# A 16x16 block inverse by substitution in place of four doubling levels, with its blocks moved through DRAM

## The chip, the cores and the metric

One core of one Trainium2 chip runs the whole program. The metric is the device time of one execution in microseconds (us). TensorE (PE) does matmuls and transposes, VectorE (DVE) and ScalarE (ACT) elementwise work, GpSimd (POOL) elementwise work and indirect transfers; SyncE (SP) issues most DMAs, ACT some. Each engine runs its own instruction stream in order and waits on semaphores.

## What is computed

One decoder layer for 512 prompt tokens and 32 sample tokens: an input projection, a gated DeltaNet branch, a forgetting-attention branch, gates and an output projection, and a mixture of 64 experts. The change is mostly in the DeltaNet recurrence over the prompt, in chunks of 64 tokens:

```python
lmat = beta[..., :, None] * jnp.einsum('nbhik,nbhjk->nbhij', k, k) * dec_strict
gam = jnp.exp(big_g)
rhs = beta[..., None] * jnp.concatenate([v, gam[..., None] * k], axis=-1)
sol = lax.linalg.triangular_solve(lmat, rhs, left_side=True, lower=True, unit_diagonal=True)
...
def step(s, xs):
    w1c, w2c, qgc, aqkc, kdc, glc = xs
    u = w1c - jnp.einsum('bhck,bhkv->bhcv', w2c, s)
    o = jnp.einsum('bhck,bhkv->bhcv', qgc, s) + jnp.einsum('bhij,bhjv->bhiv', aqkc, u)
    s = glc[..., None, None] * s + jnp.einsum('bhck,bhcv->bhkv', kdc, u)
    return s, o
```

`lmat` is strictly lower triangular, so the solve needs the inverse of a unit triangular 64x64 matrix for each chunk and head.

## The kernel before

The program is a row of blocks with a barrier of all engines between them. The block of the DeltaNet recurrence (L1347 and on, 447 to 761 us) works through four tiles of 128 tokens (two chunks each), all eight heads at once. For a tile, TensorE does in order:

- 16 transposes of keys and queries (L1362), the decay rows (L1367) and key-key and key-query products (L1371). DVE and ACT then make the decay matrix (L1486, L1544) and DVE the scaled matrix LT (L1492, L1493; its last write raises `lt_done`).
- The inverse, by doubling. `Um` holds the inverse of the diagonal blocks found so far and `Tm` its transpose. Level 0 (blocks of 2) needs one set of transposes (L1385); each of levels 1 to 5 (blocks of 4 to 64) masks LT on DVE (`level_mask`, L1475), multiplies it with Tm (L1393), lets ACT copy the product out of PSUM (L1561), multiplies with Um (L1403), lets DVE subtract (L1511), and, but for the last, transposes Um (L1411) for ACT to copy (L1564).
- The weighted rows w1 and w2 (L1417, L1418, in turns), and for each chunk the recurrence (L1431, L1437 to L1439) with DVE's updates (L1519 to L1522).

Between these steps stand "later pieces": parts of products that the next blocks need (the branch gates and later modulation rows), whose place is written out by hand in `later_pieces`. There are 80 in all, 12 of them in the block before. Of the 68 in this block 54 are halves of a gate group (L1202, four matmuls of 272 columns), 7 are raw modulation products (L1197) and 7 spread those over rows (L1189). ACT copies finished groups out of two banks (`later_out`: L1238, L1225, L1230) and stores them. Their weights come in 2 MB loads that SP issues (`send_later`, L226), each when an earlier slab has been used. POOL works on the sample tokens' state all the while (L1625 to L1635, until 607 us).

Other places that the change touches: the tile of 32 sample tokens of the z projection (L682, among the sample attention), the same tile in the shared expert (L2115), and the loads of the modulation rows (`load_mod`, L1762 and L1763).

## Time and profile before

| what | us |
|---|---|
| median of 3 runs | 1658.97 |
| lowest, highest run | 1651.38, 1660.43 |
| the profiled execution's own time | 1660.09 |
| its span in the trace | 1658.1 |
| TensorE busy | 1521.5 (92%) |
| VectorE, ScalarE, GpSimd busy | 615.4, 323.4, 316.8 |
| recurrence block, barrier to barrier | 447.2 to 761.1 |

The span is what the trace covers; the execution's own time is 2.0 us more. A fp32 matmul is listed as two instructions, so x16 beside a product of eight heads is eight matmuls. A row of the timeline that merges pipelined instructions ends a little after the next one starts; the step between starts is what a piece of work takes.

### The profile page before, as it was taken

The page shows a single profiled execution, that of the slowest core. Times are in us where ns is not written, and L with a number is a line of the kernel's source. Part 1 is how long each engine was busy: PE and PEld are TensorE (multiplying, and loading weights), DVE is VectorE, ACT ScalarE, POOL GpSimd, SP SyncE. Part 2 cuts the span into 40 slices and gives each one's busy share as a digit, 9 for nine tenths or more (in the row PEclk, how much of TensorE's full clock was granted, in tenths as well). Part 3 has the DMA queues.
Part 4 walks back from the last instruction along what each step waited for, and adds up shares of the span by engine and source line. Part 5 has one row for each costly group of instructions (what it writes and reads, how often), then busy time and mean ns, then how long its engine had stood idle before and what let it go on. Part 6 is the DMA issues. An engine that isn't in the chain of part 4 may idle for free. (4 is left out here: it accounts for less than half of the span.)

```text
span 1658.1 us, 21127 instructions
## 1 busy us (share of the span) xinstructions
PE 1521.5 (92%) x8094; PEld 886.0 (53%) x8094; DVE 615.4 (37%) x1260; ACT 323.4 (20%) x701; POOL 316.8 (19%) x345
## 2 busy tenths in 40 slices
PE   5999999999989899998998779999999989999966
PEld 3866767644677777787745333444343433333322
DVE  2002554331763625333669833421111111111128
ACT  1003334332331223221102201111111111111121
POOL 7000000000169971000002510111111111111000
PEclk8999999999999999998999899999999999999978
DMA  9312111112351143306540187999999999999665
GB/s 341 125 51 97 41 52 51 52 51 77 126 152 67 60 142 120 122 10 226 194 146 30 38 317 271 395 407 414 409 422 399 400 420 411 413 385 422 260 263 237
DMA packets 103231, 357.15 MB, mean 215 GB/s; under 512 B 27243, under 2 KB 27371, under 8 KB 77011
## 3 DMA queue, kind: packets, MB, share of 16 engines
q1 hardware_dynamic: 78998, 300.80, 47.0%
q0 software_dynamic: 15520, 39.17, 6.2%
q10 hardware_dynamic: 8614, 15.84, 2.7%
q8 instruction: 65, 1.06, 0.3%
q14 instruction: 34, 0.28, 0.0%
HBM read 330.70 MB, written 37.64 MB: 222 GB/s over the span
## 5 line engine op out<-in xcount | busy, mean ns | idle before, releaser
L1991 PE MATMUL bank<-arena 128*32 128x512 f32 (+2 forms) x1536 | 334.7, 611 | 23.5 <-DMA arena<-in_w_up 23.5
L1991 PEld LDWEIGHTS bank<-arena 128*32 128x32 f32 (+2 forms) x1536 | 119.1, 138 | 206.5 <-issue 206.2
L1999 PE MATMUL bank<-arena 128*32 128x512 f32 (+2 forms) x768 | 168.6, 598 | 0.7 <-DVE arena L2733 0.7
L2727 DVE TENSOR_TENSOR arena<-arena,bank 128x256 f32<-128x256 f32 x46 | 19.4, 421 | 324.0 <-ACT arena L2385 324.0
L1978 POOL DMA_INDIRECT expert_rows<-arena x46 | 46.5, 1010 | 486.0 <-PE bank L1984 419.5
L1202 PE MATMUL bank<-arena 128*128 128x272 f32 x512 | 129.7, 401 | 0.4 <-ACT arena L1238 0.4
L438 PE MATMUL bank<-arena 128*128 128x272 f32 x480 | 113.0, 398 | 4.7 <-DVE arena L1860 2.4
L1999 PEld LDWEIGHTS bank<-arena 128*32 128x32 f32 (+2 forms) x768 | 55.0, 134 | 110.3 <-issue 109.4
L1202 PEld LDWEIGHTS bank<-arena 128*128 128x128 f32 x512 | 94.7, 193 | 24.2 <-ACT arena L1238 3.8
L438 PEld LDWEIGHTS bank<-arena 128*128 128x128 f32 x480 | 92.1, 193 | 25.1 <-DVE arena L1860 3.2
L668 PE MATMUL bank<-arena 128*128 128x272 f32 x384 | 100.3, 405 | 0.0
L455 PE MATMUL bank<-arena 128*128 128x512 f32 (+3 forms) x304 | 84.8, 437 | 3.3 <-ACT arena L2331 2.4
L2385 ACT ACTIVATE arena<-bank 128x256 f32<-128x256 f32 x46 | 17.7, 384 | 347.5 <-PE bank L1991 347.5
L2739 DVE COPY arena<-bank 128x512 f32<-128x512 f32 x46 | 31.8, 692 | 126.8 <-PE bank L1999 126.8
L668 PEld LDWEIGHTS bank<-arena 128*128 128x128 f32 x384 | 70.2, 193 | 16.0 <-issue 3.6
L455 PEld LDWEIGHTS bank<-arena 128*128 128x128 f32 (+1 forms) x304 | 45.3, 187 | 41.4 <-issue 36.8
L1607 POOL TENSOR_TENSOR arena<-arena 128x512 f32<-128x512 f32 x5 | 6.8, 1354 | 290.5 <-POOLq L1243 290.2
L2447 POOL DMA_INDIRECT expert_lists<-arena x34 | 35.6, 1046 | 137.8 <-DVE arena L2573 128.4
L1984 PE MATMUL bank<-arena 128*128 128x128 f32 x368 | 49.5, 279 | 9.0 <-DMA arena<-h_rows,arena 9.0
L2391 ACT COPY arena<-bank 128x512 f32<-128x512 f32 x46 | 27.0, 587 | 152.4 <-PE bank L1999 152.4
L1974 POOL DMA_INDIRECT arena<-h_rows,arena x46 | 47.0, 1023 | 44.0 <-DVE arena L1918 24.0
L1393 PE MATMUL bank<-arena 128*128 128x128 f32 x320 | 42.1, 283 | 12.7 <-DVE arena L1508 7.4
(469 smaller groups left out, 2124.8 us busy)
## 6 DMA issues: line engine op xcount, KB each, us to landing
arena<-in_w_gate SPq DMA_DIRECT2D x64, 1024.0 KB, 12.5
arena<-in_w_up SPq DMA_DIRECT2D x64, 1024.0 KB, 16.6
arena<-in_w_down SPq DMA_DIRECT2D x64, 1024.0 KB, 15.5
arena<-in_w_ada SPq DMA_DIRECT2D x12, 2048.0 KB, 10.3
arena<-in_w_in SPq DMA_DIRECT2D x11, 2048.0 KB, 8.7
arena<-expert_rows SPq DMA_DIRECT2D x8, 2048.0 KB, 25.5
gate_logits<-arena ACTq DMA_DIRECT2D x16, 272.0 KB, 2.3
arena<-gate_logits SPq DMA_DIRECT2D x8, 544.0 KB, 5.2
```

Source lines behind the costliest of these rows:

```text
L438: mm = nc.tensor.matmul(pair[i][:, 0:HALF], w[:, k, m * P:(m + 1) * P], rhs[:, k, i * HALF:(i + 1) * HALF], start=k == 0, stop=k == kt - 1)
L455: mm = nc.tensor.matmul(out, lhs[:, k, t * P:t * P + n], w[:, k, cols], start=k == 0, stop=k == kt - 1)
L668: mm = nc.tensor.matmul(out[:, 0:HALF], w[:, k, (m % 4) * P:(m % 4 + 1) * P], hT[:, k, half * HALF:(half + 1) * HALF], start=k == 0, stop= ...
L1202: mm = nc.tensor.matmul(out[:, 0:HALF], w[:, k, m * P:(m + 1) * P], hT[:, k, half * HALF:(half + 1) * HALF], start=k == 0, stop=k == KD - 1)
L1393: mm = nc.tensor.matmul(bank[hb][:, col(h)], Lm[:, h, :], Tm[:, h, :], start=True, stop=True)
L1974: return nc.gpsimd.indirect_dma_start(out=into, out_offset=None, in_=h2_d, in_offset=bass.IndirectOffsetOnAxis(ap=rows, axis=0), bounds_ch ...
L1978: return nc.gpsimd.indirect_dma_start(out=y_d, out_offset=bass.IndirectOffsetOnAxis(ap=rows, axis=0), in_=of, in_offset=None, bounds_check ...
L1984: mm = nc.tensor.transpose(bank[half][:, k * P:(k + 1) * P], of[:, kk * P:(kk + 1) * P], ident)
L1991: mm = nc.tensor.matmul(out[rows].rearrange("p (a n) -> p a n", a=2), x[:, k, rows], gate_up_slot(n)[:, :, k, :], start=k == 0, stop=k == ...
L1999: mm = nc.tensor.matmul(out[rows, :], h[:, k, rows], down_slot(n)[:, k, 512 * half:512 * half + 512], start=k == 0, stop=k == 1)
L2447: scat.inc(nc.gpsimd.indirect_dma_start(out=list_rows, out_offset=bass.IndirectOffsetOnAxis(ap=adi[:, t, k:k + 1], axis=0), in_=tokval[:, ...
L2739: nc.vector.tensor_copy(Yb[u % RY][:, 512:D], bank[6][:, :]).then_inc(y_v.sem, 1)
```

## The change

- The masks for the levels (`lvl`, 24 GpSimd instructions) go. Levels 0 to 3 of the inverse go with them.
- In their place the eight diagonal blocks of 16x16 of LT, for eight heads, are inverted by forward substitution on DVE. For that the blocks are stored to DRAM (`key_blocks`: eight stores, the even blocks on SP's queue, the odd ones on ACT's), loaded back with one block and head per partition (two loads), and the result `x16` goes the same way back (two stores of `key_block_inverses`, eight loads into `Um`). The substitution is 15 steps of a product and a subtraction on `xp` in PSUM and one copy, 31 instructions, each waiting for the one before.
- Two levels stay (blocks of 32 and of 64). Their blocks of LT are copied by ACT into zeroed tiles instead of being masked on DVE.
- Keys and decays of tile t+1 are made before the weighted rows of tile t, and the substitution for tile t+1 stands between the two chunks of tile t on DVE. The 68 later pieces are placed anew.
- The decay rows use both halves of the array in turns; the weighted rows are eight matmuls of one kind and then eight of the other.
- Products for 32 tokens (z, the shared expert, the modulation rows) are done in four column groups of 32 rows instead of at 512 columns. The modulation rows go to DRAM unexpanded, and their loads take five DMAs instead of two; two of the four sets are issued by SP behind the first two gate loads instead of by ACT.

```diff
-    lvl = const(6, P)
+    gqT_odd, n16 = const(CW, P), const(16, 16)
...
+    n16_d = nc.dram_tensor("key_blocks", (NB, H, 16, 16), F32).ap()
+    x16_d = nc.dram_tensor("key_block_inverses", (NB, H, 2, 8, 16), F32).ap()
-    NL = 6
+    xp = bank[2][:, 0:128].rearrange("p (r i) -> p r i", r=8)
+    NL = 2
...
+            def block_inverses(t):
+                dve.wait_ge(xp_made.sem, t + 1)
+                dve.wait_ge(n16_in.sem, 32 * (t + 1))
+                for j in range(15):
+                    n = 15 - j
+                    row = xp[:, :, j:j + 1].to_broadcast([P, 8, n])
+                    step(nc.vector.tensor_tensor(p16[:, :, 0:n], row, n16[:, j:j + 1, j + 1:16].to_broadcast([P, 8, n]), ALU.mult))
+                    step(nc.vector.tensor_tensor(xp[:, :, j + 1:16], xp[:, :, j + 1:16], p16[:, :, 0:n], ALU.subtract))
+                done(x16_done, nc.vector.tensor_copy(x16[:, :, 1:16], xp[:, :, 1:16]))
...
+            later_pieces(pe, "state before", 2)
+            keys_and_decays(0)
+            for t in range(PT):
+                levels(t)
+                if t + 1 < PT:
+                    keys_and_decays(t + 1)
+                weighted_rows(t)
+                states(t, 0)
+                later_pieces(pe, (t, "state between"), (4, 4, 3, 1)[t])
+                states(t, 1)
...
+                for a in range(1, NB, 2):
+                    b16 = slice(16 * a, 16 * a + 16)
+                    n16_odd_out.inc(act.dma_start(n16_d[a].rearrange("h j i -> j h i"), LT[b16, :, b16]), 16)
...
+            def store_key_blocks(t):
+                sp.wait_ge(lt_done.sem, t + 1)
+                for a in range(0, NB, 2):
+                    b16 = slice(16 * a, 16 * a + 16)
+                    n16_out.inc(sp.dma_start(n16_d[a].rearrange("h j i -> j h i"), LT[b16, :, b16]), 16)
+            def load_key_blocks(t):
+                sp.wait_ge(n16_out.sem, 8 * NB * (t + 1))
+                sp.wait_ge(n16_odd_out.sem, 8 * NB * (t + 1))
+                for g in range(2):
+                    n16_in.inc(sp.dma_start(n16[64 * g:64 * g + 64], n16_d.rearrange("a h j i -> (a h) j i")), 16)
+            def move_block_inverses(t):
+                sp.wait_ge(x16_done.sem, t + 1)
+                for g in range(2):
+                    x16_out.inc(sp.dma_start(x16_d[:, :, g].rearrange("a h r i -> (a h) r i"), x16[64 * g:64 * g + 64]), 16)
+                sp.wait_ge(x16_out.sem, 32 * (t + 1))
+                for a in range(NB):
+                    b16 = slice(16 * a, 16 * a + 16)
+                    um_in.inc(sp.dma_start(Um[b16, :, b16], x16_d[a].rearrange("h g r i -> (g r) h i")), 16)
...
-                for k in range(KD):
-                    mm = nc.tensor.matmul(out, hT[:, k, t * P:t * P + n], ws[0][:, :, k, :], start=k == 0, stop=k == KD - 1)
+                for k in range(KD):
+                    for q in range(4) if t == PT else ():
+                        mm = nc.tensor.matmul(out[QUAD * q:QUAD * q + QUAD, 0:P], hT[:, k, SEQ:TOK], ws[0][:, q // 2, k, P * (q % 2):P * (q % 2) + P],
+                                              start=k == 0, stop=k == KD - 1)
```

The order on TensorE in one level of the inverse of a tile, before; four more such groups follow or precede it (L1393: product with Tm, L1403: with Um, L1202: a later piece, L1411: transposes of Um):

```order
L1393 MATMUL bank<-arena 128x128 [waits later_inverse_T_copied,level_masked]
L1393 MATMUL bank<-arena 128x128 x3
L1393 MATMUL bank<-arena 128x128 [waits later_inverse_T_copied,level_masked]
L1393 MATMUL bank<-arena 128x128 x3
L1403 MATMUL bank<-arena 128x128 [waits LT_product_copied]
L1403 MATMUL bank<-arena 128x128 x3
L1403 MATMUL bank<-arena 128x128 [waits LT_product_copied]
L1403 MATMUL bank<-arena 128x128 x3
L1202 MATMUL bank<-arena 128x272 [waits later_loaded1]
L1202 MATMUL bank<-arena 128x272 x3
L1411 MATMUL bank<-arena 128x128 [waits inverse_updated]
```

The order on TensorE now, where the second tile's inverse begins (line numbers are those of the changed kernel: L1198 and L1203 are later pieces, L1399 the transposes of Um, L1407 and L1412 the two products of a level):

```order
L1198 MATMUL bank<-arena 32x512 [waits later_loaded1,later_product_copied]
L1198 MATMUL bank<-arena 32x512 x7
L1203 MATMUL bank<-arena 128x272 [waits later_loaded0,later_product_copied]
L1203 MATMUL bank<-arena 128x272 x3
L1399 MATMUL bank<-arena 128x128 [waits o_copied,block_inverses_loaded]
L1399 MATMUL bank<-arena 128x128 x7
L1407 MATMUL bank<-arena 128x128 [waits inverse_T_copied,level_blocks_copied]
L1407 MATMUL bank<-arena 128x128 x3
L1407 MATMUL bank<-arena 128x128 [waits inverse_T_copied]
L1407 MATMUL bank<-arena 128x128 x3
L1412 MATMUL bank<-arena 128x128 [waits LT_product_copied]
L1412 MATMUL bank<-arena 128x128 x3
```

Five levels have become two, and the inverse starts with a wait for the loads of the block inverses, with two later pieces ahead of it.

On SP, the loads of weights (L227; L226 before) now stand between the small transfers. The first tile's part of the queue, where before were only the three L226 rows:

```order
L227 DMA arena<-in_w_in 128x8x512 [waits later_product]
L1667 DMA key_blocks<-arena 16x8x16 [waits LT_done]
L1667 DMA key_blocks<-arena 16x8x16 x3
L1673 DMA arena<-key_blocks 64x256 [waits odd_key_blocks_stored,key_blocks_stored]
L1673 DMA arena<-key_blocks 64x256
L227 DMA arena<-in_w_ada 128x8x512 [waits later_product] x2
L1678 DMA key_block_inverses<-arena 64x128 [waits block_inverses_done]
L1678 DMA key_block_inverses<-arena 64x128
L1682 DMA arena<-key_block_inverses 16x8x16 [waits block_inverses_stored]
L1682 DMA arena<-key_block_inverses 16x8x16 x7
L227 DMA arena<-in_w_in 128x8x512 [waits later_product]
```

Two weight loads stand between the block loads and the stores of the inverses, and each waits for a later piece on TensorE.

## Rows read from the trace of the kernel before

**Rows 1.** The page, part 1: busy us, share of the span, instructions.

```profile
PE 1521.5 (92%) x8094; PEld 886.0 (53%) x8094; DVE 615.4 (37%) x1260; ACT 323.4 (20%) x701; POOL 316.8 (19%) x345
```

**Rows 2.** Windows: the recurrence block; busy PE, PEld, DVE, ACT, POOL, clock, DMA.

```profile
447.20:761.10 313.90, 295.89 (x2208) 238.11 (x2208) 149.84 (x219) 82.80 (x184) 150.16 (x102) 0.97 0.28 91
```

**Rows 3.** Timeline of PE: start, duration, line; one level of the first tile.

```profile
481.77 2.02 PE L1393 MATMUL bank<-arena 128*128 128x128 f32 x16 [0.33 <-ACT arena L1564]
483.63 2.00 PE L1403 MATMUL bank<-arena 128*128 128x128 f32 x16
485.47 2.00 PE L1202 MATMUL bank<-arena 128*128 128x272 f32 x8
487.31 1.04 PE L1411 MATMUL bank<-arena 128*128 128x128 f32 x8
488.67 2.02 PE L1393 MATMUL bank<-arena 128*128 128x128 f32 x16 [0.33 <-ACT arena L1564]
```

**Rows 4.** Timeline of PE: the weighted rows' first and last, then chunk one.

```profile
508.12 0.43 PE L1417 MATMUL bank<-arena 128*128 128x64 f32 x2
...
513.94 2.10 PE L1202 MATMUL bank<-arena 128*128 128x272 f32 x8
515.97 0.68 PE L1431 MATMUL bank<-arena 64*64 64x64 f32 x16
...
520.62 2.10 PE L1202 MATMUL bank<-arena 128*128 128x272 f32 x8
```

**Rows 5.** Timeline of PE: the head of a tile, at full clock and after a wait.

```profile
454.16 2.05 PE L1367 MATMUL bank<-arena 8*128 8x128 f32 x16
456.14 2.00 PE L1371 MATMUL bank<-arena 64*128 64x256 f32 x16
458.07 5.77 PE L1202 MATMUL bank<-arena 128*128 128x272 f32 x24
...
530.91 3.65 PE L1362 MATMUL bank<-arena 128*128 128x128 f32 x16 [2.56 <-DVE arena L1526]
534.35 3.30 PE L1202 MATMUL bank<-arena 128*128 128x272 f32 x8
```

**Rows 6.** Timeline of DVE: from small to large instructions, and held ones.

```profile
432.74 0.19 DVE L1272 COPY arena<-bank 128x32 f32<-128x32 f32 x1
432.97 0.18 DVE L1273 TENSOR_SCALAR arena<-arena 128x32 f32<-128x32 f32 x1
...
464.50 0.43 DVE L1493 TENSOR_TENSOR arena<-bank,arena 128x256 f32<-128x256 f32 x1
...
469.30 4.00 DVE L1506 TENSOR_TENSOR arena<-arena 128x512 f32<-128x512 f32 x1
...
479.24 1.41 DVE L1475 TENSOR_TENSOR arena<-arena,bank 128x512 f32<-128x512 f32 x2
```

**Rows 7.** Timeline of SP: small stores, and the next load that waits for them.

```profile
447.44 8.33 SPq L1580 DMA_DIRECT2D sample_rows<-arena  x24
457.02 0.68 SPq L1586 DMA_DIRECT2D arena<-in_state_ssm  x1
```

**Rows 8.** DMA issues, 400 to 770 us: size each, median time to landing.

```profile
arena<-in_w_in SPq DMA_DIRECT2D x3, 2048.0 KB, 8.6
arena<-sample_out POOLq DMA_DIRECT2D x8, 8.0 KB, 2.1
arena<-in_x_sample SPq DMA_DIRECT2D x1, 128.0 KB, 13.5
sample_out<-arena POOLq DMA_DIRECT2D x2, 32.0 KB, 8.2
```

**Rows 9.** Timeline of PE: 32-token products at 512 columns, and in quarters.

```profile
407.54 3.62 PE L682 MATMUL bank<-arena 128*32 128x512 f32 x8
...
902.29 1.96 PE L448 MATMUL bank<-arena 128*32 128x128 f32 x64
...
973.00 7.05 PE L2115 MATMUL bank<-arena 128*32 128x512 f32 x16
```

More of the change, by code:

```diff
@@ L1064, in take_z @@
                 n, src = TOKS[t], filled(act, ("z", t))
-                read(("z", t), nc.scalar.activation(z_tm[0:n, t, :], src[0:n, :], ACT.Silu))
+                for rows, cols in QUARTERS if t == PT else [(slice(0, P), slice(0, W))]:
+                    ins = nc.scalar.activation(z_tm[0:n, t, cols], src[rows, 0:cols.stop - cols.start], ACT.Silu)
+                    ach.inc(ins) if cols.stop < W else read(("z", t), ins)
             for b in range(DB):
@@ L1188, in later_piece @@
             pe.wait_ge(fill_rd.sem, GROUP_OF[("raw", p[1])] + 1)
-            fill_mm.inc(nc.tensor.matmul(out[0:1 + NS_TOK, :], sel33, raw, start=True, stop=True))
+            for rows, cols in QUARTERS:
+                mm = nc.tensor.matmul(out[rows, 0:P], sel9, raw[:, cols], start=True, stop=True)
+            fill_mm.inc(mm)
             return
@@ L1373, in _, with levels @@
                 kk_mm.inc(mm)
-                later_pieces(pe, (t, "decay"), 3)
-                later_pieces(pe, (t, "masks"), 2)
+                later_pieces(pe, (t, "decay"), 14 if t == 0 else 4)
+            def levels(t):
+                later_pieces(pe, (t, "inverse back"), 2)
+                pe.wait_ge(um_in.sem, 16 * NB * (t + 1))
+                if t:
+                    pe.wait_ge(o_sb.sem, t)
+                for hb in range(2):
+                    for h in range(4 * hb, 4 * hb + 4):
+                        mm = nc.tensor.transpose(bank[hb][:, col(h)], Um[:, h, :], ident)
+                    t_mm.inc(mm)
@@ new lines, in _ @@
+            for i in range(2):
+                scaled_rows(0, i)
+            done(s_zero, nc.vector.memset(S, 0.0))
+            step(nc.vector.memset(Um, 0.0))
+            for Lm in Lm_of:
+                done(lm_zero, nc.vector.memset(Lm, 0.0))
+            for i in range(2, 5):
+                scaled_rows(0, i)
+            keys_and_decays(0)
+            dve.wait_ge(i16_made.sem, 2)
+            step(nc.vector.tensor_copy(x16[:, :, 0:1], i16[:, :, 0:1]))
+            block_inverses(0)
@@ new lines, in _ @@
+            for t in range(PT):
+                q = hd(qkv_tm[:, t, 0:W])
+                if t + 1 < PT:
+                    scaled_rows(t + 1, 0)
+                    scaled_rows(t + 1, 1)
+                inverse_level(t, 0)
+                if t + 1 < PT:
+                    for i in range(2, 5):
+                        scaled_rows(t + 1, i)
+                inverse_level(t, 1)
+                if t + 1 < PT:
+                    keys_and_decays(t + 1)
+                dve.wait_ge(w_mm.sem, t + 1)
+                done(w1_sb, nc.vector.tensor_copy(rows_of[t % 2][:, 0], bank[4].ap()))
+                if t + 1 < PT:
+                    step(nc.vector.memset(Um, 0.0))
+                states(t, 0)
+                if t + 1 < PT:
+                    block_inverses(t + 1)
+                states(t, 1)
@@ new lines, in _ @@
+            later_out(act, "state before")
+            keys_and_decays(0)
+            for t in range(PT):
+                if 0 < t < PT - 1:
+                    act.wait_ge(o_sb.sem, t)
+                    scales_to_psum(t + 1)
+                later_out(act, (t, "inverse back"))
+                take_T(t, 0)
+                take_P1(t, 0)
+                later_out(act, (t, "level"))
+                take_T(t, 1)
+                take_P1(t, 1)
+                if t + 1 < PT:
+                    keys_and_decays(t + 1)
@@ L1603, in _ @@
             step = chained(pool, gch)
+            for g in range(2):
+                half = i16[64 * g:64 * g + 64]
+                step(pool.memset(half, 0.0))
+                i16_made.inc(pool.affine_select(out=half, in_=half, compare_op=ALU.not_equal, fill=1.0, base=8 * g,
+                                                pattern=[[1, 8], [-1, 16]], channel_multiplier=0))
+            pool.wait_ge(i16_made.sem, 2)
             for t in range(NT):
```

350 lines of the change are left out of this document (180 added, 170 removed).

## The prediction, made before the changed kernel ran

> **What bounds the kernel now.** I read the shares first [rows 1]: TensorE is busy 92% of the span, the others 37% and less, so what counts is TensorE's own work and its waits. Then the window of the recurrence block [rows 2]: 313.9 us, TensorE busy 295.9, clock 0.97. The timeline shows what it does there. One level of the inverse goes from 481.77 to 488.67, 6.90 us [rows 3]: first product 1.86, second 1.84, a later piece 1.84, transposes and a short wait for ACT 1.36. Nothing in a level waits for long; DVE and ACT are hidden. So removed matmuls should show nearly in full, as long as what takes their place is hidden too.
>
> I count the block as work plus rest. Per tile: transposes 1.8, decay rows 1.98 and key products 1.93 [rows 5], first transposes 0.9, five levels of 3.70, four sets of transposes of 0.95, the weighted rows 5.82 (508.12 to 513.94), and twice 0.61 + 1.95 for the chunks (the gaps between pieces in [rows 4]): 39.8, four times is 159. The 68 later pieces: 54 at 1.84, 7 raw ones at 1.86, 7 of rows at 0.98, together 119. Work 278.6, so the rest (waits, half clock, tail) is 35.3 of the 313.9.
>
> **TensorE's work after.** Three of five levels go: 3 x (3.70 + 0.95) = 13.9 us per tile. The weighted rows take 0.364 per matmul in turns; alone, a product of eight takes 0.23 each [rows 3], and 16 of them 3.9: 1.9 saved (an estimate, since a change of tile shape is what I blame; between nothing and 3.0). The decay rows with both halves in turns: between 0 and 0.98 saved, I take 0.6, as 64-row products (L1371) do run two at a time, 256 columns in the time that 128 take alone. The seven row pieces become four matmuls in four column groups, about 0.3 instead of 0.98: 4.8 in all. Sum 4 x 16.4 + 4.8 = 70.4; work after 208.2.
>
> **The chain that replaces it.** From `lt_done` of a tile to its inverse on TensorE: four stores per queue at 0.35 each (8.33 for 24), 1.25 from the end of the last issue to the next instruction that waits for them [rows 7]; two loads 0.7 + 2.1, the landing of the small load [rows 8]; the substitution; two stores 0.7 + 1.3; eight loads 2.8 + 2.1. A DVE instruction costs 0.15 + 0.00104 per element (0.19 at 32 columns, 0.43 at 256, the gap to the next 0.04) [rows 6]. The 30 of the substitution have 8n elements, n from 15 to 1, twice 960 in all: 2.0 + 30 x 0.19, and the copy 0.3, 8.1 us (bound: 12, if such short strided forms take 0.4 each). The Trainium skill (DMA: Bandwidth & Descriptors, "Anatomy of one DMA") puts the fixed cost of any DMA at about 2.0 us, mostly the receipt of the write. By it both store legs would be 0.7 longer and the sum about 6 us higher; the store row here says 1.25, the load row agrees.
>
> The substitution of tile t+1 stands on DVE behind the first chunk of tile t, so it starts when that is done, about 10.3 after `lt_done` (3.9 + piece + 0.61 + 1.84 + 1.95 + DVE), when its blocks have long arrived (5.5). It ends at 18.4, its result is back at 25.3. TensorE in that time has weighted rows 3.9, two chunks of 2.56, and 9 later pieces, 25.0 together. So the chain is just covered: a wait of 1 us per tile. DVE is in the substitution when the second chunk's product comes, at 0.1, 1.3 and 2.9 us too late where 4, 4 (one short) and 3 pieces stand between: 4.3. A step of one store less in issue (ACT takes the odd ones) is 1.4 us per tile on a leg that has 4.8 us to spare: nothing.
>
> **The first tile is the weak place.** Its chain starts at TensorE's key products plus 6.9 (458.07 to 464.93 [rows 5, 6]), beside 14 pieces. ACT empties the banks of the pieces only after its four stores and seven copies, about 4.3 us after `lt_done`, while TensorE runs out of free banks after 3 pieces: a wait of 7.7. The weights of the fifth raw piece are loaded only after the block loads are issued: 8.6 us [rows 8], a wait of 3.2. The next slab's load goes out when that piece is done, and the stores of the inverses are queued behind its 2 MB: the small load behind a big one took 13.5 [rows 8]. I get the inverse back 5.7 after TensorE is ready. After a wait of 2.56 the next 24 instructions took 6.95 instead of 3.97 [rows 5], at the clock's lower level, so I add 3.0 once, behind the 5.7; behind the two other waits the chain hides it.
>
> Rest after: first keys 1.2, banks 7.7, slab 3.2, inverse of the first tile 5.7 and clock 3.0, copies inside the levels 4 x 1.0, `lt_done` and subtraction 1.5, inverses of the others 3.0, second chunks 4.3, last tile without cover 2.0, one or two DVE instructions held 3.0 (next part), tail as before 2.6: 41.2. Block 208.2 + 41.2 = 249.4, that is 64.5 less.
>
> **DVE beside GpSimd.** An instruction with both inputs in SBUF took 4.00 instead of 0.69 beside GpSimd; with one in PSUM two took 1.41 as ever [rows 6]. The substitution keeps `xp` in PSUM, so each of its 30 has one. The Trainium skill (SBUF — State Buffer, "SBUF: two separate sides") states it as a lock: a DVE instruction with two SBUF inputs, or GpSimd's, holds the shared ports for its whole length. By that rule too the 30 are free, but the scaling of the state is not; the trace agrees, and GpSimd is busy to 607, over the first two tiles.
>
> **Outside the block.** The z tile of 32 tokens: 8 of its 16 instructions take 3.62, the whole some 7.4; in quarters 64 instructions took 1.96 [rows 9]. Of the 5.5 saved part only uncovers DVE and ACT steps of the sample attention that these products hid (about 2 us each turn): 3.0. The shared expert's: 7.05 becomes 2.0; DVE's next step before the expert lists waits for exactly it, and ends 4.5 earlier. The fewer masks are on GpSimd, idle long before the first barrier: nothing; if it were the last there, 10 us. The modulation loads by SP go before a 2 MB load and five issues take 1.1 more than two; what waits for them has slack, nothing (bounds -1, +3). Everything after is the expert phase, whose loads start when the ranks are known, so it moves as a whole.
>
> **Sum**, against the profiled execution's 1660.1: -64.5 - 3.0 - 4.5 = -72, 1588. That execution is 1.1 above the median of the three runs shown, so it is nearly the same against both.
>
> **Rivals.**
> - The chain is longer than its cover by some 8 us per tile (substitution at 12, legs at 2.6 instead of 1.3 and 2.1 with more issue time). The cover has no slack, so all of it shows, three or four times: 1588 + 34 = 1622. For it: 25.3 against 25.0 is close, and no row shows 16x16 blocks in DRAM. Against: the rows for small DMAs and DVE are plain.
> - Slower: the small transfers queue behind weight loads and state stores. 32 KB stores of the sample output took 8.2 and the load behind 2 MB 13.5 [rows 8]. With stores at 8.2 and loads at 13.5 the chain is 57, 32 above its cover; four times, less the 9 already counted, 1588 + 119 = 1707. It decides from a chain of 43 on, where the 72 are used up. Against: outside the first tile the weight loads are issued early enough to be landed.
> - The gain is given back: the expert phase waits for weights, not for routing, 1655. Against: the loads of the first experts wait for the order of ranks.
> - GpSimd holds the substitution after all (in the first two tiles, 30 x up to 3.3 us, chain at 40 or more): 1640.
> - The first tile's waits are hidden better and tile shape changes cost more than I think: 1572.
>
> **How the numbers follow.** Forecast 0.68, own range 1574 to 1606 (the 41.2 of rest by a third, weighted rows by 1 us a tile, z and shared by 2). Longer chain 0.18, slower 0.04, given back 0.03, held by GpSimd 0.03, better 0.04. A measurement of this kernel tells about 0.5%, 8.3 us, from no change. Faster 0.68 + 0.18 + 0.03 + 0.04 = 0.93; within 0.5% 0.03; slower 0.04. The range reaches from 1572 to the longer chain, 1622.
>
> **What would show it.** The recurrence block at about 249 us; 31 DVE instructions in 8 us with gaps of 0.04; a period of some 53 us per tile; TensorE's wait for the loads of `Um` near 1 us in tiles 2 to 4 and near 6 in the first; the shared expert's last tile in 2 us. Wrong would be: waits for these loads of over 5 us in every tile, clock below 0.9 in the block (many waits of 2.5 us each cost 3 more), or substitution steps above 0.35.

## The result, and the profile after

| | before | after |
|---|---|---|
| median of 4 runs, same chip | 1655.18 | 1580.02 |
| lowest, highest | 1646.45, 1660.43 | 1572.22, 1582.13 |
| profiled execution, its span | 1660.1, 1658.1 | 1579.5, 1577.7 |

The ratio is 0.954, 95% interval 0.949 to 0.960: faster by 75 us (forecast 1588, range 1572 to 1622). In spans, stage by stage:

| stage | before | after | change | forecast |
|---|---|---|---|---|
| up to the recurrence block (z tile) | 447.2 | 443.9 | -3.3 | -3.0 |
| recurrence block | 313.9 | 246.9 | -67.0 | -64.5 |
| output norm, gates | 74.4 | 72.3 | -2.1 | 0 |
| routing and shared expert | 158.5 | 152.6 | -5.9 | -4.5 |
| expert phase to the end | 664.0 | 662.0 | -2.0 | 0 |

The page, part 1, for the changed kernel, beside [rows 1]:

```profile
PE 1435.3 (91%) x7758; PEld 825.9 (52%) x7758; DVE 578.1 (37%) x1304; ACT 304.8 (19%) x682; POOL 304.6 (19%) x325
```

The window of the recurrence block, in the columns of [rows 2]:

```profile
443.90:690.80 246.90, 217.84 (x1770) 174.27 (x1770) 112.92 (x262) 63.58 (x160) 150.51 (x106) 0.97 0.39 121
```

TensorE is busy 78.1 us less there (295.9 to 217.8), and idle 11.1 us more (18.0 to 29.1). No run below puts the levels back; that three of them went is read from this count of work. Where TensorE waits now, in its timeline: the first tile's banks (the PSUM banks that ScalarE has to empty) and slab (a 2 MB load of weights), then the block inverses of tiles one, two and three, and the second chunk's additions on DVE in the third tile, for tile four's substitution stands before them there (lines of the changed kernel: L1399 transposes `Um`, L1450 needs the additions of L1526).

```profile
467.57 13.65 PE L1203 MATMUL bank<-arena 128*128 128x272 f32 x48 [7.67 <-ACT arena L1240]
482.83 1.92 PE L1198 MATMUL bank<-arena 128*32 128x512 f32 x16 [1.61 <-DMA arena<-in_w_ada]
...
498.11 1.09 PE L1399 MATMUL bank<-arena 128*128 128x128 f32 x8 [3.25 <-DMA arena<-key_block_inverses]
...
552.31 1.09 PE L1399 MATMUL bank<-arena 128*128 128x128 f32 x8 [0.57 <-DMA arena<-key_block_inverses]
...
605.25 1.09 PE L1399 MATMUL bank<-arena 128*128 128x128 f32 x8 [1.59 <-DMA arena<-key_block_inverses]
...
651.98 0.27 PE L1450 MATMUL bank<-arena 64*64 64x64 f32 x1 [3.06 <-DVE arena L1526]
```

From tile one's inverse to tile two's it is 54.2 us (forecast some 53). The first, and the last two, of the 31 DVE instructions of a substitution, 8.2 us from 474.42 to 482.61 (forecast 8.1):

```profile
474.42 0.28 DVE L1509 TENSOR_TENSOR arena<-bank,arena 128x120 f32<-128x120 f32 x1 [11.79 <-DMA arena<-key_blocks]
...
482.12 0.17 DVE L1510 TENSOR_TENSOR bank<-bank,arena 128x8 f32<-128x8 f32 x1
482.33 0.28 DVE L1511 COPY arena<-bank 128x120 f32<-128x120 f32 x1
```

The weighted rows, now all of w1 and then all of w2, in PE's timeline: 2.84 us from 525.86 to 528.70, where [rows 4] has 5.82. The row piece behind them is down to 0.4:

```profile
525.86 1.89 PE L1428 MATMUL bank<-arena 128*128 128x64 f32 x16
527.68 1.09 PE L1430 MATMUL bank<-arena 128*64 128x128 f32 x16
528.70 0.43 PE L1189 MATMUL bank<-arena 128*32 128x128 f32 x8
```

SP's timeline in the first tile: start and time of issue. The block inverses leave (485.25) when the queue gets past the weight loads, 2.6 us after the substitution is done.

```profile
462.73 2.18 SPq L1667 DMA_DIRECT2D key_blocks<-arena  x4
470.82 1.89 SPq L1673 DMA_DIRECT2D arena<-key_blocks  x2
473.92 11.29 SPq L227 DMA_DIRECT2D arena<-in_w_ada  x2
485.25 1.23 SPq L1678 DMA_DIRECT2D key_block_inverses<-arena  x2
493.03 3.69 SPq L1682 DMA_DIRECT2D arena<-key_block_inverses  x8
```

And the DMA issues of the block, size each and median time to landing, beside [rows 8]:

```profile
arena<-key_blocks SPq DMA_DIRECT2D x8, 64.0 KB, 2.2
arena<-key_block_inverses SPq DMA_DIRECT2D x32, 8.0 KB, 1.7
...
key_blocks<-arena ACTq DMA_DIRECT2D x16, 8.0 KB, 1.7
key_blocks<-arena SPq DMA_DIRECT2D x16, 8.0 KB, 1.7
key_block_inverses<-arena SPq DMA_DIRECT2D x8, 32.0 KB, 2.1
```

### The profile page after: what moved, and what is told of

Its sections match the earlier page's. It is cut to its first block and busy times, and to the rows that moved or that the text cites. A ratio compares the mean times of both kernels' runs of the same rounds, so it can differ in the third digit from the quotient of the medians.

```text
span 1577.7 us, 20481 instructions
## 1 busy us (share of the span) xinstructions
PE 1435.3 (91%) x7758; PEld 825.9 (52%) x7758; DVE 578.1 (37%) x1304; ACT 304.8 (19%) x682; POOL 304.6 (19%) x325
## 5 line engine op out<-in xcount | busy, mean ns | idle before, releaser
L1203 PE MATMUL bank<-arena 128*128 128x272 f32 x512 | 129.4, 406 | 8.9 <-ACT arena L1240 8.6
L1203 PEld LDWEIGHTS bank<-arena 128*128 128x128 f32 x512 | 96.9, 195 | 35.1 <-ACT arena L1240 10.8
L434 PEld LDWEIGHTS bank<-arena 128*128 128x128 f32 x480 | 92.2, 193 | 23.8 <-issue 2.8
L451 PE MATMUL bank<-arena 128*128 128x512 f32 (+3 forms) x304 | 90.3, 458 | 2.5 <-ACT arena L2452 2.0
L664 PEld LDWEIGHTS bank<-arena 128*128 128x128 f32 x384 | 70.3, 193 | 15.9 <-issue 3.6
L451 PEld LDWEIGHTS bank<-arena 128*128 128x128 f32 (+1 forms) x304 | 48.7, 200 | 42.8 <-issue 39.0
L2572 POOL DMA_INDIRECT expert_lists<-arena x34 | 32.7, 963 | 138.5 <-DVE arena L2698 129.0
L2100 PE MATMUL bank<-arena 128*128 128x128 f32 x368 | 49.5, 279 | 7.2 <-DMA arena<-h_rows,arena 7.2
L2100 PEld LDWEIGHTS bank<-arena 128*128 128x128 f32 x368 | 43.4, 145 | 8.4 <-issue 8.4
## 6 DMA issues: line engine op xcount, KB each, us to landing
arena<-in_w_gate SPq DMA_DIRECT2D x64, 1024.0 KB, 12.5
```

What stands on the lines that cost most here:

```text
L434: mm = nc.tensor.matmul(pair[i][:, 0:HALF], w[:, k, m * P:(m + 1) * P], rhs[:, k, i * HALF:(i + 1) * HALF], start=k == 0, stop=k == kt - 1)
L451: mm = nc.tensor.matmul(out, lhs[:, k, t * P:t * P + n], w[:, k, cols], start=k == 0, stop=k == kt - 1)
L664: mm = nc.tensor.matmul(out[:, 0:HALF], w[:, k, (m % 4) * P:(m % 4 + 1) * P], hT[:, k, half * HALF:(half + 1) * HALF], start=k == 0, stop= ...
L1203: mm = nc.tensor.matmul(out[:, 0:HALF], w[:, k, m * P:(m + 1) * P], hT[:, k, half * HALF:(half + 1) * HALF], start=k == 0, stop=k == KD - 1)
L2100: mm = nc.tensor.transpose(bank[half][:, k * P:(k + 1) * P], of[:, kk * P:(kk + 1) * P], ident)
L2572: scat.inc(nc.gpsimd.indirect_dma_start(out=list_rows, out_offset=bass.IndirectOffsetOnAxis(ap=adi[:, t, k:k + 1], axis=0), in_=tokval[:, ...
```

## The experiments

Each is the changed kernel with one edit, or with several of them together where the text says so. The block is measured in each trace from its first later piece on TensorE (the 32-row products that start at 444.09 in the change) to the next stage's first product (690.87). The ratio is to the kernel before, run beside it. That kernel's own median moved between 1648.8 and 1656.0 from one group of runs to the next, so differences of a few us are read from the traces, of which there is one for each kernel.

| kernel | median, us | ratio, 95% interval | block, us |
|---|---|---|---|
| the change | 1580.0 | 0.954, 0.949 to 0.960 | 246.8 |
| all stores on SP | 1576.3 | 0.954, 0.948 to 0.959 | 245.5 |
| weighted rows in turns | 1594.6 | 0.964, 0.959 to 0.970 | 263.4 |
| new order on SP | 1575.9 | 0.954, 0.949 to 0.959 | 244.5 |
| the same, banks emptied early | 1573.5 | 0.952, 0.946 to 0.957 | 240.7 |
| `xp` in SBUF | 1624.7 | 0.985, 0.982 to 0.988 | 294.7 |
| 7 of 15 steps | 1572.6 | 0.955, 0.952 to 0.959 | 239.4 |
| inverses stored twice | 1601.2 | 0.971, 0.967 to 0.975 | 266.4 |
| 32-token tiles at 512 columns | 1592.6 | 0.967, 0.964 to 0.970 | 247.2 |
| all on SP, new order | 1572.3 | 0.952, 0.946 to 0.958 | 239.5 |
| paused substitution | 1588.6 | 0.960, 0.953 to 0.966 | 261.6 |
| all three | 1573.8 | 0.952, 0.948 to 0.957 | 240.5 |
| paused, state stores held | 1593.0 | 0.963, 0.958 to 0.968 | 251.1 |

Inside the block, TensorE's stretches in us: from the first piece to the first tile's inverse (the first L1399), from there to the second tile's, and so on, and from the fourth to the next stage:

| kernel | to the first | to the second | to the third | to the fourth | rest |
|---|---|---|---|---|---|
| the change | 54.0 | 54.2 | 52.9 | 54.1 | 31.5 |
| all stores on SP | 53.4 | 52.6 | 52.4 | 55.5 | 31.7 |
| new order on SP | 49.8 | 55.2 | 52.3 | 55.7 | 31.5 |
| the same, banks emptied early | 50.1 | 52.8 | 52.9 | 53.3 | 31.5 |
| all on SP, new order | 49.8 | 51.5 | 52.0 | 54.6 | 31.5 |
| 7 of 15 steps | 54.2 | 54.1 | 50.1 | 49.7 | 31.3 |
| inverses stored twice | 56.5 | 57.5 | 63.1 | 57.8 | 31.5 |
| paused, state stores held | 54.2 | 54.6 | 52.8 | 56.8 | 32.7 |

The kernels of the third and fourth row run the same instructions behind the first inverse, and still differ there by 2.4 us twice. So 1 or 2 us of block between two traces prove nothing by themselves.

### The stores' queue

```diff
-                for a in range(1, NB, 2):
-                    b16 = slice(16 * a, 16 * a + 16)
-                    n16_odd_out.inc(act.dma_start(n16_d[a].rearrange("h j i -> j h i"), LT[b16, :, b16]), 16)
...
-                for a in range(0, NB, 2):
+                for a in range(NB):
```

> All eight stores of a tile's key blocks go out on the sync queue, none on ScalarE's. Theory (the block load comes back some 5 us before VectorE is free to use it, except in the first tile, where it waits behind a 2 MB load anyway): the block loads are issued about 1.8 us later, the substitution of tiles 2 to 4 starts when it did, and the recurrence block stays at 247 us within 1.5. Rival (the stores lie on the chain): 1.8 us for each of four tiles, block at 254. A second rival: ScalarE, freed of 1.8 us of issues per tile, empties the banks sooner in the first tile, and the 7.7 us wait there becomes 5.7; block at 245.

ScalarE gets to the banks sooner: TensorE's wait for them is 5.63 us instead of 7.67, the wait for the next slab 3.03 instead of 1.61, and that for the first inverse 2.29 instead of 3.25. The block is 1.3 us shorter, the time not to be told apart. So giving ScalarE half of the stores gains nothing: SP's eight stores take 3.63 us instead of 1.72 for four (second tile), but the substitution waits for DVE to finish the first chunk anyway. It has a cost that the theory left out. On ScalarE the four stores and three groups of copies stand before its copy of w2 (L1638), and TensorE waits for that copy before the first chunk (L1444); the profile names no releaser and calls the wait "issue". The first such place in the change, on the way to the second inverse:

```profile
526.06 1.81 ACTq L1593 DMA_DIRECT2D key_blocks<-arena  x4
...
530.25 0.60 ACT L1638 ACTIVATE arena<-bank 128x512 f32<-128x512 f32 x1
...
530.94 0.68 PE L1444 MATMUL bank<-arena 64*64 64x64 f32 x16 [1.81 <-issue]
```

and with all stores on SP:

```profile
527.55 0.68 PE L1444 MATMUL bank<-arena 64*64 64x64 f32 x16 [0.51 <-DVE arena L1556]
```

On the way to the second, third and fourth inverse this wait is 1.81, 0.27 and 0.97 us in the change. In the three kernels with all stores on SP the first is 0.51 and the others are absent; in the ten with stores on ScalarE the first is 1.8 each time, except with the weighted rows in turns (0.50), where TensorE itself comes later.

### The shape of the matmuls

```diff
                     nc.tensor.matmul(bank[4][:, HD * h:HD * h + HD], Um[:, h, :], rows4[:, 3, HD * h:HD * h + HD], start=True, stop=True)
-                for h in range(H):
```

> The weighted rows are again multiplied in turns, a 128x64 product and a 64-column one for each head, as in the kernel before. Theory: the turns cost 5.8 us instead of 2.85 per tile, since the two shapes cannot follow one another closely; the stage stands on TensorE's path and on the way to VectorE's first chunk, so all of 4 x 3.0 = 12 us shows, block at 259. Rival: the stage is cover for the transfers of the next tile's blocks, so waits for them shrink by as much and under 5 us show.

In turns the weighted rows take 5.82 us again, 3.0 more a tile, 12 in all. The other 4.6 of the 16.6 us are in the main one wait, 5.2 longer than in the change, less the 1.3 by which the first wait for ScalarE is shorter. In PE's timeline:

```profile
616.04 1.97 PE L1399 MATMUL bank<-arena 128*128 128x128 f32 x8 [6.75 <-DMA arena<-key_block_inverses]
```

That the third tile alone lost 5 us here is taken up below. The 32-token tiles:

```diff
-            for rows, cols in QUARTERS if t == PT else [(slice(0, P), slice(0, W))]:
-                mm = nc.tensor.matmul(out[rows, 0:cols.stop - cols.start], hT[:, k, t * P:t * P + n], w[:, k, cols],
...
+            mm = nc.tensor.matmul(out[0:n, :], hT[:, k, t * P:t * P + n], w[:, k, :], start=k == 0, stop=k == KD - 1)
```

> The edit: the 32-token tile of the z product and of the shared expert's first product go back to 512 columns with 32 rows out, instead of four products of 128 or 256 columns in the four quarters of the array. Theory: the z tile is 3.3 us longer and the shared expert's 4.5 to 5.9, all of it TensorE's own time, so 1588 within 2, ratio to the changed kernel 1.005; the recurrence block stays at 246.9 within 1.5. Rival: in the shared expert's stage the routing work on DVE ends last and the gain there came from it, so that only the z tile's 3.3 us come back: 1583.

The block kept its 247 us, and the whole took 12.5 us more by the medians and 21 by the ratios (0.967 against 0.954), either good to about 10. TensorE's own share can be read off: the z tile is 7.42 us of matmuls instead of 2.37, the shared expert's 7.05 instead of 1.96, 10.1 together. What of it shows is read inside the traces. Before the z tile TensorE is 0.9 us ahead of the change's (410.36 against 411.26), behind it 4.0 late (422.73 against 418.72): 4.9 us. From the end of the block to the first expert's products (L2096; L2100 in the change) it is 230.1 us instead of 224.9: 5.2. Both come back whole, so the rival (3.3 alone) falls, and the z tile is worth 5 us rather than 3. The start of the block can't show this: in the kernels here that share all code up to it, it lay anywhere from 438.7 to 447.7.

### The substitution beside GpSimd

```diff
-    xp = bank[2][:, 0:128].rearrange("p (r i) -> p r i", r=8)
+    xp = x16
```

> The edit: the substitution adds its rows up in the SBUF buffer of the inverses instead of a PSUM bank; the copy out of the bank at its end becomes a copy of the same size between two SBUF buffers, whose target nobody reads, so the result is the full one. Theory: in the first two recurrence tiles GpSimd still works on its own stage, and a DVE instruction with both operands in SBUF has to share a port with it; the substitution of 8.2 us takes well over 10 us there (15 is the bound that the 31 instructions allow by the DVE instructions that were held in the kernel before) and stays within 0.5 us of 8.2 in tiles three and four, where GpSimd is idle. The inverse of the first tile then comes 2 to 7 us later, the time is 1582 to 1592. Rival one: nothing is held, all four stay at 8 to 8.5 us, the time is that of the changed kernel, 1580 within 3. Rival two: an operand in SBUF is cheaper than one in PSUM, 31 instructions save about 0.06 us each, 2 us of the chain, and the time is 1577 to 1579.

The theory's mechanism holds and its price was far too low: 33.4 and 34.2 us in the first two tiles, 8.0 in the third. DVE and, under it, GpSimd in this kernel:

```profile
479.78 0.27 DVE L1509 TENSOR_TENSOR arena<-arena 128x104 f32<-128x104 f32 x1
480.08 3.58 DVE L1510 TENSOR_TENSOR arena<-arena 128x104 f32<-128x104 f32 x1
483.70 0.26 DVE L1509 TENSOR_TENSOR arena<-arena 128x96 f32<-128x96 f32 x1
483.99 3.57 DVE L1510 TENSOR_TENSOR arena<-arena 128x96 f32<-128x96 f32 x1
...
489.52 4.42 DVE L1510 TENSOR_TENSOR arena<-arena 128x64 f32<-128x64 f32 x1
```

```profile
479.78 3.76 POOL L1744 TENSOR_TENSOR arena<-arena 128x2048 f32<-128x2048 f32 x1
483.64 5.54 POOL L1745 TENSOR_SCALAR arena<-arena 128x2048 f32<-128x2048 f32 x1
489.26 4.59 POOL L1746 TENSOR_TENSOR arena<-arena 128x2048 f32<-128x2048 f32 x1
```

Nine of the 31 instructions take over 1 us. The one of 480.08 ends with GpSimd's of 479.78, that of 489.52 with that of 489.26; each new instruction of GpSimd holds another one. The lock that the Trainium skill states (SBUF — State Buffer, "SBUF: two separate sides") says this; the run agrees, but for GpSimd's TENSOR_SCALAR of 5.54 us, beside which DVE was let go after 3.57 and did six more instructions unheld (the profile's spans for GpSimd are rough). TensorE waited 20 us for the first tile's inverse, the kernel lost 45 us, and some 26 of the change's 75 are left. So the PSUM operand carries more of the gain than the place of any store.

### What the first tile waits for

```diff
                 dve.wait_ge(n16_in.sem, 32 * (t + 1))
-                for j in range(15):
+                for j in range(7):
```

> The edit: only the first 7 of the 15 steps of the substitution are done; the last 8 rows of every block inverse are left out, the instructions left are as before. Theory: the chain of the four tiles is shortened by about 3.5 us each (8.2 to 4.7), which takes away the wait for the inverse in tile one (3.25 us and the 1.5 us at half clock behind it) and that in tile two (0.6), and most of the 4.8 us in which TensorE waits for DVE's second-chunk copy; the time falls by 5 to 9 us, to 1571 to 1575. Rival: only the first tile's inverse is on the path, the rest waits for something else: 3 us, 1577, and the waits for DVE stay at 4 to 5 us.

The substitution took 4.43 us, the time fell by 7.4, as the theory said, yet not where it said. From the block's first piece to the first inverse it was 54.16 us against 54.02, with the wait still there, in PE's timeline:

```profile
496.73 1.09 PE L1399 MATMUL bank<-arena 128*128 128x128 f32 x8 [3.45 <-DMA arena<-key_block_inverses]
```

and in SP's:

```profile
472.17 11.45 SPq L227 DMA_DIRECT2D arena<-in_w_ada  x2
483.67 1.23 SPq L1678 DMA_DIRECT2D key_block_inverses<-arena  x2
```

The result lay ready at 477.4, and SP sat at a weight load until 483.7. In the first tile the queue's order sets the end, later DVE does: TensorE's waits for the additions fell from 4.8 us to 0.7, the third inverse came without a wait, and the stretches to the third and fourth inverse are 2.9 and 4.4 us shorter. The order is changed by itself:

```diff
-            send_later(3)
             store_key_blocks(0)
+            send_later(3)
             load_key_blocks(0)
             send_later(4)
-            send_later(5)
             move_block_inverses(0)
+            send_later(5)
```

> Only the order on the sync queue in the first tile: the stores of the key blocks go ahead of the first 2 MB weight load, and the inverses' stores and loads ahead of the third. Theory (the first tile's chain is late because it queues behind 2 MB twice): key blocks are back near 467 instead of 474, the inverse near 485 instead of 498, and TensorE is then held only by its own pieces; it begins the inverse at about 492.6 instead of 498.1 (times of the changed kernel's trace), block 5.5 us shorter, 241. Rival (TensorE's free banks and slabs hold the first tile, not the chain): under 2 us.

The first inverse came 49.84 us after the first piece, 4.2 earlier, without a wait; the block was only 2.3 us shorter, as the stretches to the second and fourth inverse were 1.0 and 1.5 longer. With one group of banks emptied by ScalarE before `lt_done` as well:

```diff
+                else:
+                    later_out(act, "first banks")
                 act.wait_ge(lt_done.sem, t + 1)
```

> The same order on the sync queue, and ScalarE empties the first two groups of later pieces of the first tile before it waits for the masked matrix, instead of after its stores and copies. Theory: the 7.7 us wait for free banks goes, but 4 to 5 of it come back as a wait for the weights of the next slab, which land at about 472; 2 us more than the order alone, block at 239. Rival: nothing beyond the order alone, since the slab decides.

The wait for banks went, and the slab took it over whole:

```profile
475.76 9.45 PE L1203 MATMUL bank<-arena 128*128 128x272 f32 x32 [8.98 <-DMA arena<-in_w_in]
```

The two waits together were 9.4 us with the order alone, this one is 9.0, and the first inverse came no sooner (50.13 us after the first piece, 49.84 before). The block is 3.8 us shorter, but in the stretches to the second and fourth inverse, which the edit leaves alone. So the theory's number was met and its mechanism was not seen; that emptying banks early is worth anything is not shown. The two cheap edits together:

> Two edits together: all eight stores of key blocks from the sync queue, and in the first tile the queue's order of the run with the new order (the stores ahead of the first weight load, the block inverses ahead of the third). Theory: each alone gave 1.3 and 2.3 us of the block (245.5 and 244.5 against 246.8), on waits that are not the same (the banks that ScalarE empties, the inverse of the first tile), so together 243 to 244 and 1574 to 1577. Rival: both shorten the same stretch and the slab of weights takes the difference, the block stays at 244.5 to 245.5, and the wait for the slab rises from 1.6 to 3 us or more.

Block 239.5, 7.3 shorter than the change's and 3.7 more than the two edits' sum; the waits for slabs did rise, from 1.6 to 7.8 us, so the rival's sign was there, but the three waits for inverses fell from 5.4 to 1.9. In the first tile the stores' queue adds nothing to the order (49.8 us both). The stretch to the second inverse is 2.7 us shorter than the change's: 1.3 is the wait for ScalarE, which is gone here as in the other kernels with all stores on SP, the rest is not accounted for. It has the lowest median of the kernels that leave nothing out, 1572.3. Its ratio to the kernel before, 0.952, can't be told from the change's 0.954.

### Is there any slack?

```diff
-                sp.wait_ge(x16_out.sem, 32 * (t + 1))
+                sp.wait_ge(x16_out.sem, 64 * t + 32)
+                for g in range(2):
+                    x16_out.inc(sp.dma_start(x16_d[:, :, g].rearrange("a h r i -> (a h) r i"), x16[64 * g:64 * g + 64]), 16)
+                sp.wait_ge(x16_out.sem, 64 * (t + 1))
```

> The edit: the block inverses are stored twice, the second store sent when the first has landed, then loaded back as before; the chain gets longer by one store leg, 0.6 us of issue and 2.1 us of landing, 2.7 to 3.5 us a tile, and no engine but the sync queue has more work. Theory: the work that covers the chain has nothing left over in tiles one and two and about 1.5 us in three and four, as the 3.25 and 0.57 us of waiting for the inverses show; the added leg is paid with 3 + 3 + 2 + 2 us and some of it at the half clock, the time is 1588 to 1594, and the waits for the inverses add up to 14 to 17 us instead of 5.4. Rival one: other work moves into the gap, the time rises by under 4 us. Rival two: each wait lets the clock fall, and the price is half as much again, 1596 or more.

```profile
500.16 1.97 PE L1399 MATMUL bank<-arena 128*128 128x128 f32 x8 [5.74 <-DMA arena<-key_block_inverses]
...
557.67 1.97 PE L1399 MATMUL bank<-arena 128*128 128x128 f32 x8 [3.19 <-DMA arena<-key_block_inverses]
...
620.78 1.97 PE L1399 MATMUL bank<-arena 128*128 128x128 f32 x8 [7.17 <-DMA arena<-key_block_inverses]
```

The waits add up to 16.1 us, 10.7 more, but the block got 19.7 longer. The other 9.2 us are busy time (227.0 against 217.8 us in the block, mean clock 0.92 against 0.97): behind these waits eight transposes take 1.97 us where they take 1.09 in the change's rows, at a granted clock of 0.50, the engine's lower level of 1.2 GHz.

By its total this is rival two. But the tiles differ: the stretches to the four inverses are 2.5, 3.3, 10.2 and 3.7 us longer. The added leg takes 2.4 to 2.7 us in each tile (SP's rows). In the third tile it was 7.95 us from the first pair of stores to the second, where it is 2.44 in the fourth: the first pair ran into two large stores of GpSimd's, of which the next section speaks. With the third stretch priced like its neighbours, some 3.5, the block would be 13 us longer and the time 1593, inside the theory's range. That is an estimate; no run stores twice without the collision.

### The pause, and the state's stores

```diff
                 for j in range(15):
+                    if j == pause:
+                        new_values(t - 1, 1)
...
-                    block_inverses(t + 1)
-                states(t, 1)
+                    block_inverses(t + 1, (15, 11, 8)[t])
+                states(t, 1, early=0 < t < PT - 1)
```

> The edit: in tiles two and three DVE pauses the substitution of the next tile (after 11 and after 8 of its 15 steps) for the two additions of the second chunk that TensorE waits for, and then goes on. Theory: the waits of TensorE for these additions fall from 4.8 us to under 1.5, as they did to 0.7 where half of the substitution was left out, while the chain gets 0.9 us longer, which tile three pays in its wait for the inverse (1.6 becomes 2.5) and tile four has to spare: the block 3 us shorter, 244, the time 1576 to 1578. Rival: what waits is only moved from the additions to the inverses, the block stays at 246 to 247.5.

The waits for the additions fell to 1.1 us, and the block grew by 14.8, in the trace of the slowest of its four runs (1580.0 to 1596.2). Fourth tile: no wait for additions, but 4.82 for its inverse, with the lower clock behind it. It looks like the same idle time, moved to the end of the cover, in one piece. Part of it is something else: in the last run of this section, with 4.73 there, the fourth tile's substitution starts 40.1 us after the third inverse instead of 37.6, behind work at the lower clock, and takes 9 us instead of 8.2. Third tile: 9.28 us, and for this SP and POOL (its DMA issues) show the cause:

```profile
605.96 1.10 SPq L1685 DMA_DIRECT2D key_block_inverses<-arena  x2
608.39 9.33 SPq L1689 DMA_DIRECT2D arena<-key_block_inverses  x8
```

```profile
606.28 1.87 POOL L1761 DMA_DIRECT2D out_ssm_sample<-arena  x1 [0.33 <-POOL arena L1757]
608.75 1.68 POOL L1761 DMA_DIRECT2D out_ssm_sample<-arena  x1
```

GpSimd ends its stage with two stores of 512 KB of state. The issue of tile three's eight small loads against them, in all thirteen kernels:

| kernel | loads from | state stores from | issue of the eight |
|---|---|---|---|
| all on SP, new order | 591.9 | 603.6 | 4.2 |
| 7 of 15 steps | 594.0 | 601.7 | 5.1 |
| new order on SP | 594.8 | 602.4 | 3.9 |
| all three | 595.0 | 605.7 | 3.6 |
| paused, state stores held | 595.3 | 600.9 | 3.7 |
| banks emptied early | 596.7 | 607.1 | 3.9 |
| all on SP | 596.8 | 603.8 | 4.1 |
| the change | 599.2 | 603.1 | 3.9 |
| 512 columns | 606.0 | 608.7 | 3.6 |
| in turns | 604.8 | 603.6 | 9.6 |
| paused | 608.4 | 606.3 | 9.3 |
| inverses stored twice | 615.7 | 602.6 | 3.6 |
| `xp` in SBUF | 648.9 | 607.3 | 4.2 |

Ahead of the stores the loads take 3.6 to 5.1 us, in the two kernels that issue them just behind the stores' start 5.5 us more, and again 3.6 and 4.2 once the stores have landed (7.9 to 9.4 us after their issue). With the inverses stored twice their first store was hit: 2.11 us of issue and 5.8 to the next instruction instead of 1.10 and 1.3. The change itself comes through with nothing to spare: its eighth load is issued by 603.09, the first state store at 603.10. The Trainium skill (DMA: Bandwidth & Descriptors, "Queues, rings and completion order") states that each DMA engine takes turns between queues packet by packet; the loads were indeed not shut out, only issued at some 0.4 of the pace.

All three edits together:

> All stores on the sync queue, the new order of that queue in the first tile, and the paused substitution, in one kernel. Theory: the three work on different waits (banks, the first tile's inverse, the second chunk's additions), so the block is 246.8 - 1.3 - 2.3 - 3 = 240 and the time 1571 to 1574, ratio to the changed kernel 0.995 to 0.997. Rival: with two of them gone the third wait is covered by what is left, the block is 243 or more and the time 1575 or more.

Block 240.5, time 1573.8: the pause adds nothing to the two others (239.5, 1572.3). TensorE's wait for the third inverse is 3.44 us here, without the state stores near, 1.04 without the pause. In the fourth tile the wait for the inverse is 0.55 here, with one of 2.28 for a slab before it.

The last run was to show the state stores' part by taking them out of the way:

```diff
+            pool.wait_ge(um_in.sem, 48 * NB)
             for half in range(2):
```

> The edit: the paused substitution as before, and GpSimd's stores of the sample state (two of 512 KB, in that run issued at 606.3 and 608.8 us) wait until the third tile's block inverses are loaded. In the run with the paused substitution alone the eight loads of the third tile were issued at 608.4 and took 9.3 us instead of 3.6, and TensorE waited 9.3 us for them; in the changed kernel the same loads were issued from 599.2 to 603.1 and the state stores began at 603.1. Theory: it is these stores that hold the small loads; with them behind, the issue of the eight loads takes 3.6 to 4.1 us in the third tile, the wait for them falls from 9.3 to 2 to 3 us, the block from 261.6 to 244 to 250, and the time to 1575 to 1582, with the four runs within 6 us of each other instead of 16. Rival: the pause itself makes the third tile's chain late, the wait stays at 6 us or more and the time at 1585 or more.

The place did what the theory said: issue 3.65 us, wait 2.56 instead of 9.28, block 251.1 instead of 261.6, just above the 244 to 250; tile four's wait is still 4.73. The time did not: 1593.0, four runs from 1584.0 to 1604.0. The trace is of the fastest of them, where the pause's was of its slowest, so the two blocks are further apart than the kernels. What the other three lost is in no trace. So that the state stores slow the small loads is shown by the table and this trace; that they are why the paused kernel is slow and its runs scatter is not, and the scatter stays open.

## Why the prediction was right, and by how much it was off

**Right: the count of TensorE's work.** It had 70.4 us of matmuls fewer and 5.9 of idle and slow time more. Measured: 78.1 busy less, 11.1 idle more. The work is off by 7.7 and the idle time by 5.2 the other way, so that 67.0 comes so near to 64.5 is in part luck (a part of the busy time also passes at the lower clock).

**Mis-sized terms.** The weighted rows were put at 3.9 us, and took 2.84; the run with them in turns showed that the order of tile shapes is what costs (12 us of work of the 78 come from that loop alone). The upper bound, 3.0 saved, was the right value. Four tiles of it explain 4.2 of the 7.7 by which the work term was short; the decay rows, 0.99 saved a tile instead of 0.6 (515.60 to 516.59), explain 1.6 more. Of the waits: banks 7.67 (7.7 foreseen), second chunks 4.8 (4.3), other inverses 2.2 (3.0), copies in the levels 3.0 (4.0), first inverse 3.25 (5.7), slab 1.61 (3.2), the clock behind the first inverse 1.5 (3.0; 3.57 us for 16 instructions of L1407 instead of 2.02). The first inverse was foreseen with its stores queued behind a 2 MB load, and that leg did take 7.8 us (485.25 to 493.03 in SP's rows); why the sum still came out 2.4 lower was not taken apart.

**A term left out.** The stores on ScalarE were weighed only as part of the chain (1.4 us on a leg with 4.8 to spare: nothing). That leg had the time, but the engine had not: TensorE's waits for ScalarE's copy of w2 behind these stores, 3.05 us in all where they are 0.51 with the stores on SP, are in no term of the 41.2.

**The store leg.** The forecast took 1.25 from the end of issue. The Trainium skill (DMA: Bandwidth & Descriptors, "Anatomy of one DMA") has about 2.0 for a whole DMA, fitted on GpSimd's path; these stores are SP's. The inverses' stores took 1.33 from the end of issue (third tile) and 1.80 (second), so the row was the better guide and still short. The chain from the substitution's start to the inverse was 16.1 us in tile two against 15.0.

**"The cover has no slack"** is what the doubled store shows: 2.4 to 2.7 us more of chain cost 2.5, 3.3 and 3.7 us in the stretches to the first, second and fourth inverse, so it showed in full, with work at the lower clock on top. Of the third's 10.2, 5.5 are the collision with the state stores. The "longer chain" rival's chance of 0.18 was for a chain that did not occur.

**GpSimd.** The rival "holds the substitution" had 30 times up to 3.3 us as bound, 1640; with `xp` in SBUF it would have been right (1624.7). In PSUM nothing was held, as forecast.

**The slower rival** (small transfers behind weight loads and state stores) had its mechanism right and the change mostly slips past it: its own first tile has a store leg of 7.8 us, which was counted, and in the edited kernels a store of 5.8 and loads of 9.3 us occur, though in one tile and not in four.

**Outside the block.** The shared expert's tile is 1.96 us, as forecast from [rows 9]; its stage gained 5.9 instead of 4.5. The z tile was put at 3.0; the reverse edit gives 4.9. That the stage up to the block gained only 3.3 all the same is within the scatter of its end (438.7 to 447.7). The 2.1 in output norm and gates and 2.0 at the end were not foreseen and were not tried.

## What to carry to other kernels

When a chain on slow queues replaces matmuls, compare its length with the work that covers it: here the cover had no slack, and 2.5 us more of chain cost 2.5 to 3.7 a tile, as work behind the longer waits ran at the lower clock. Before making the chain's arithmetic faster, look for what shares the queue or the DMA engines at that moment (here a weight load ahead in SP's order, and a big store at the end of GpSimd's work), and for what stands behind an issue on the same engine (here ScalarE's copy behind its stores). Where a chain of short DVE instructions runs beside GpSimd, give it a PSUM operand. And compare kernels tile by tile: two traces of the same code differed by 2.4 us in a tile, and a total hides where the time went.

## What was not expected of the hardware

- A chain of 31 short DVE instructions with both operands in SBUF beside GpSimd took 33.4 us instead of 8.2, over twice the 15 that the row of one held instruction suggested: each of GpSimd's instructions holds one anew.
- Two 512 KB state stores stretch the issue of eight loads of 8 KB on another queue from 3.6 to 9.3 us.
- Two matmul shapes in turns cost 5.82 us for 16 matmuls, in two runs of eight 2.84.
